# A hybrid encoder layer on one core: operands on 128-byte starts, meta rows in one operand, attention stage rearranged

## The reference

```python
h = concatenate([meta, x])                       # 16 + 512 rows
n = rmsnorm(h)
proj = n @ w_in                                  # 1024 x 3912: rq rk rv rg dq dk dv iq ik iw
ret = silu(rg) * groupnorm(retention(rope(rq), rope(rk), rv))     # 4 heads of 128, chunk-causal decay
isc = sum_h iw_h * relu(rope(iq_h) @ rope(ik))                    # indexer, 8 heads of 64
att = softmax over the 128 keys with the highest isc, 8 heads of 128; then @ w_uv
h  += concatenate([ret, att]) @ w_out            # 1024 x 1024
m = rmsnorm(h)
# PEER: product keys choose 16 of 128 x 128 experts for each of 8 heads and each row
h  += sum_e gelu(m . u_e) * gate_e * v_e
out = rmsnorm(h)[16:]
```

## Time and profile before

| | us |
|---|---|
| runs | 1708.06 (1706.65 to 1708.62) |
| profiled execution | 1707.09 |
| its span, first to last instruction | 1705.3 |
| mean granted TensorE clock | 0.997 |
| projection, to about | 235 |
| retention, attention, output, FFN norm, to about | 400 |
| routing with 24 up tiles, to about | 610 |
| up tiles, to | 1172 |
| down tiles, to | 1697 |

### The profile page before, as it was taken

The page is one execution under the profiler, slowest core; times in us unless marked ns, Lnnn a source line. Parts: engine busy times, 40 slices in busy tenths (PEclk is TensorE's granted clock), DMA queues, the critical chain, the costliest instruction groups (busy, mean ns, idle before and its releaser), DMA issues.

```text
span 1705.3 us, 23289 instructions
## 1 busy us (share of the span) xinstructions
PE 1681.4 (99%) x7773; PEld 1382.8 (81%) x7773; DVE 1102.3 (65%) x2966; ACT 576.7 (34%) x900; POOL 918.8 (54%) x855
## 2 busy tenths in 40 slices
PE   9999998999999999999999999999999999999998
PEld 8867876788888888888888888888888888888886
DVE  4269867456788854444444444434788888888887
ACT  5343235244323222222222222224333333333333
POOL 3654300005433037777777777763777777767710
PEclk9999999999999999999999999999999999999999
DMA  5322141044769444444456444455999999999991
GB/s 177 107 64 74 37 101 51 13 149 174 263 236 315 148 149 148 143 148 143 142 166 232 144 147 143 142 167 189 386 390 369 374 367 357 379 372 361 375 337 53
DMA packets 183250, 351.04 MB, mean 206 GB/s; under 512 B 35664, under 2 KB 118992, under 8 KB 183024
## 3 DMA queue, kind: packets, MB, share of 16 engines
q1 hardware_dynamic: 118400, 255.47, 44.5%
q0 software_dynamic: 34816, 67.41, 11.0%
q10 hardware_dynamic: 29952, 27.28, 4.9%
HBM read 289.04 MB, written 61.02 MB: 205 GB/s over the span
## 4 chain that ended last, share of the span: by engine, by line
PE 80%; DVE 2%; issue 2%; POOL 1%; ACT 1%; DMA 0%; DVEq 0%; POOLq 0%; ACTq 0%
PE psum L274 25%; PE psum L276 25%; PE psum L275 25%; PE psum L1078 1%; PE psum L1086 1%; PE psum L1100 1%; POOL ts_lo_wq L1623 1%; PE psum L1785 1%; PE psum L1129 1%; DVE att_masked L1341 0%; POOL cand L2034 0%; POOL ts_lo_u L1623 0%; DVE mixed L1325 0%; PE psum L1114 0%; PE psum L1142 0%
## 5 line engine op out<-in xcount | busy, mean ns | idle before, releaser
L2436 POOL DMA_INDIRECT gate_map<-gate_total,gate_at x384 | 403.6, 1051 | 200.7 <-DVE same_expert L2131 110.1
L274 PE MATMUL psum<-x_hi,ts_hi_u 128*128 128x512 f32 x1024 | 399.0, 390 | 1.8 <-POOL ts_lo_u L1623 1.1
L276 PE MATMUL psum<-x_hi,ts_lo_u 128*128 128x512 f32 x1024 | 398.4, 389 | 0.0
L275 PE MATMUL psum<-x_lo,ts_hi_u 128*128 128x512 f32 x1024 | 398.4, 389 | 0.0
L1623 DVE TENSOR_TENSOR ts_lo_u<-ts_raw_u,ts_hi_u 128x1024 fp32r<-128x1024 f32 x116 | 142.2, 1226 | 336.7 <-ACT ts_hi_u L1618 336.6
L274 PE MATMUL psum<-v_hi,c_hi 128*128 128x512 f32 x768 | 298.8, 389 | 0.0
L275 PE MATMUL psum<-v_lo,c_hi 128*128 128x512 f32 x768 | 298.8, 389 | 0.0
L276 PE MATMUL psum<-v_hi,c_lo 128*128 128x512 f32 x768 | 298.8, 389 | 0.0
L1618 ACT ACTIVATE ts_hi_u<-ts_raw_u 128x1024 fp32r<-128x1024 f32 x128 | 135.4, 1058 | 394.2 <-PE psum L276 394.2
L2331 ACT ACTIVATE v_hi<-v_raw 128x1024 fp32r<-128x1024 f32 x128 | 135.8, 1061 | 314.3 <-PE psum L276 314.3
L2424 POOL DMA_INDIRECT sparse_rows<-in_peer_v,v_row x128 | 159.4, 1245 | 126.1 <-DVE sparse_more L2166 36.4
(11 more groups left out here) (270 smaller groups left out, 2310.8 us busy)
## 6 DMA issues: line engine op xcount, KB each, us to landing
ts_raw_u<-in_peer_u SPq DMA_DIRECT2D x128, 512.0 KB, 3.6
v_raw<-in_peer_v SPq DMA_DIRECT2D x128, 512.0 KB, 6.0
gate_map<-zeros SPq DMA_DIRECT2D x32, 768.0 KB, 6.8
act_in<-up_acts SPq DMA_DIRECT2D x128, 192.0 KB, 5.7
gate_in<-gate_map SPq DMA_DIRECT2D x128, 192.0 KB, 6.6
up_acts<-ut_out_u ACTq DMA_DIRECT2D x104, 192.0 KB, 1.9
raw_in<-in_w_in SPq DMA_DIRECT2D x56, 256.0 KB, 2.7
ts_raw_wq<-in_peer_wq SPq DMA_DIRECT2D x16, 512.0 KB, 5.0
```

Source lines behind the costliest of these rows:

```text
L274: nc.tensor.matmul(out, l_hi, r_hi, start=first, stop=False)
L275: nc.tensor.matmul(out, l_hi, r_lo, start=False, stop=False)
L276: return nc.tensor.matmul(out, l_lo, r_hi, start=False, stop=last)
L2436: nc.gpsimd.indirect_dma_start(gate_cells, bass.IndirectOffsetOnAxis(places["gate_at"][:, b, j:j + 1], 0), dn.total[:, b, j:j + 1], None). ...
```

## The change

1. Starts: small filler tensors (`fill_line`) and other shapes make every fp32r operand begin at a multiple of 128 bytes: h_hi, h_lo and rk_t lose their meta columns ([.., 512] instead of 528), and the meta part of rk_t moves into an unused part of sel_bias (rk_m).
2. Meta rows: one operand meta_both holds the 16 high and the 16 low columns side by side. A meta output is two matmuls per k: both parts by w_hi (32 output rows), the high part by w_lo (16 rows). The two groups of rows are rotated alike (tables and scales have both) and are added by a matmul against `fold`, two stacked 16 x 16 unit matrices, where a transpose stood; in the retention of the meta keys both groups are kept (rows 0 to 31 of the decays), so the sum is made by the product.
3. Output projection: two tiles of k per step for blocks 0 and 1 (steps 12 to 19, 20 to 27), three for block 2 (28 to 33), by `out_step`. w_out units 7 to 15 are split one per step, in VectorE's list from step 3, in ScalarE's from step 2.
4. Retention roots: no Sqrt. VectorE makes a first guess from the bits (two operations), GpSimd three Newton steps of four operations, then -mean x root (two more); ScalarE normalises (Identity with scale and bias) in steps 3, 5, 7, 8, VectorE gates one step later. ScalarE loads the Sqrt table at step 32 for the FFN norm.

```diff
+        def fill_line(name, used, c=None, side=None):
+            sb(name, [P, -used % LINE // 4], c=c, side=side)
+        fill_line("edge", LINE - SB_TOP % LINE, side="right")
+        fold = sb("fold", [META_ROWS, META_ROWS])
...
+            fill_line("final_rest", 32 + 64, rows_ctx)
...
-                rk_t=sb_high("rk_t", [P, RET_HEADS, ROWS], c=high),
+                rk_t=sb_high("rk_t", [P, RET_HEADS, FRAMES], c=high),
...
+                rest=fill_line("dk_t_rest", 4 * ROWS, stream),
...
-                hi = sb("h_hi", [P, KT, ROWS], F32R, c=c2)
-                lo = sb("h_lo", [P, KT, ROWS], F32R, c=c2)
+                hi = sb("h_hi", [P, KT, FRAMES], F32R, c=c2)
+                lo = sb("h_lo", [P, KT, FRAMES], F32R, c=c2)
...
+            def meta_product(bank, k, s, w):
+                nc.tensor.matmul(psum[0:META_ROWS, bank, 0:w], meta_both[:, k], ws.hi[:, s, 0:w], start=(k == 0), stop=False)
+                return nc.tensor.matmul(psum[0:META, bank, 0:w], meta_both[:, k, 0:META], ws.lo[:, s, 0:w],
+                                        start=False, stop=(k == KT - 1))
...
+                    if b == NB:
+                        last = nc.tensor.matmul(out, rows_in, fold[:, 0:cols], start=True, stop=True)
...
+    def out_step(p, n):
+        return DSA_HEADS * (p + 1) + 4 + n // (2 if p < LAST - 1 else 3)
...
+        def refine_roots(g):                              
+            hs = HEAD_GROUPS[g]
+            y, v, t = rstd[:, hs], var[:, hs], ab["ret_step"][:, hs]
+            pool.wait_ge(guessed, 2 * g + 2)
+            at = ROOT_STEPS * g
+            for x in range(NEWTON):
+                nc.gpsimd.tensor_tensor(t, y, y, ALU.mult).then_inc(newton, 1)
+                pool.wait_ge(newton, at + 4 * x + 1)
...
         nc.gpsimd.memset(ret_scores[:, :, 0, :], 0.0).then_inc(padded, 1)
+        refine_roots(0)
         for i in range(UNITS):
+            if i == 3:
+                refine_roots(1)
...
+        def guess_roots(g):
+            hs = HEAD_GROUPS[g]
+            dve.wait_ge(var_done, g + 1)
+            nc.vector.tensor_scalar(halved[:, hs], var[:, hs].bitcast(U32), 1, None, ALU.logical_shift_right).then_inc(guessed, 1)
+            dve.wait_ge(guessed, 2 * g + 1)
+            nc.vector.tensor_scalar(rstd[:, hs].bitcast(U32), halved[:, hs], -1.0, ROOT_GUESS, ALU.mult, ALU.add).then_inc(guessed, 1)
...
-        def ret_sqrt(g):
-            hs = HEAD_GROUPS[g]
-            act.wait_ge(var_done, g + 1)
-            nc.scalar.activation(rstd[:, hs], var[:, hs], ACT.Sqrt).then_inc(root, 1)
+        def normalize(h):
+            act.wait_ge(newton, ROOT_STEPS * (2 if h == LAST_HEAD else 1))
+            for b in range(NB):
+                nc.scalar.activation(mixed[:, b, h * P:(h + 1) * P], sums[:, h, b * P:(b + 1) * P], ACT.Identity,
+                                     bias=ab["ret_step"][:, h, b:b + 1], scale=rstd[:, h, b:b + 1]).then_inc(normed, 1)
...
+            if i in NORMED_AT:
+                normalize(NORMED_AT.index(i))
+            if i == UNITS:
+                nc.scalar.activation(ab["unused"][:], ident[:, 0:1], ACT.Sqrt)
...
-            for u in range(2 * i - 11, 2 * i - 9):
-                if EARLY_W <= u < 2 * KT:
-                    split_hi(nc, act, ws, u, seen[u], 512)
+            if EARLY_W <= i + 5 < 2 * KT:
+                split_hi(nc, act, ws, i + 5, seen[i + 5], 512)
```

More of the change, by code:

```diff
@@ L90, in tables @@
             t[:, b] = full[b * P:(b + 1) * P]
-        t[:META, NB] = full[FRAMES:]
+        for g in range(META_PARTS):
+            t[g * META:(g + 1) * META, NB] = full[FRAMES:]
         out[name] = t
@@ L97, in tables @@
     decay = np.zeros((P, RET_HEADS, FRAMES), f)
-    decay_meta = np.zeros((META, RET_HEADS, FRAMES), f)
+    decay_meta = np.zeros((META_ROWS, RET_HEADS, FRAMES), f)
+    fold = np.tile(np.eye(META, dtype=f), (META_PARTS, META_PARTS))
     for h in range(RET_HEADS):
         decay[:, h] = np.where(seen, gamma[h] ** np.abs(n - m), 0.0) * RET_DIM ** -0.5
-        decay_meta[:, h] = gamma[h] ** (n + META - np.arange(META)[:, None]) * RET_DIM ** -0.5
+        for g in range(META_PARTS):
+            decay_meta[g * META:(g + 1) * META, h] = (
+                gamma[h] ** (n + META - np.arange(META)[:, None]) * RET_DIM ** -0.5)
     out["decay"] = decay
     out["decay_meta"] = decay_meta
+    out["fold"] = fold
     out["ident"] = np.eye(P, dtype=f)
@@ L505, in _ @@
                 load_unit(sp, ws, u, in_unit(io, u))
-            sp.dma_start(xm, io["meta_tokens"]).then_inc(meta_in, 16)
+            for g in range(META_PARTS):
+                sp.dma_start(xm[g * META:(g + 1) * META], io["meta_tokens"]).then_inc(meta_in, 16)
+            sp.dma_start(fold[:], io["fold"]).then_inc(fold_in, 16)
             sp.dma_start(rope128[:], io["rope128"]).then_inc(tables_in, 16)
@@ L529, in turn @@
                 tiles = 2 if name == "misc" else 4
+                if b == NB:
+                    pe.wait_ge(fold_in, 16)
                 for t in range(tiles):
-                    last = nc.tensor.transpose(psum[:, 4 + n % 2, t * P:t * P + r], rot[0:r, n % 2, t * P:(t + 1) * P],
-                                               ident[0:r, 0:r])
+                    cols = turned_columns(name, b)
+                    out, rows_in = psum[:, 4 + n % 2, t * P:t * P + cols], rot[0:r, n % 2, t * P:(t + 1) * P]
+                    if b == NB:
+                        last = nc.tensor.matmul(out, rows_in, fold[:, 0:cols], start=True, stop=True)
+                    else:
+                        last = nc.tensor.transpose(out, rows_in, ident[:])
                 last.then_inc(rot_turned, 1)
@@ L950, in mix_rows @@
     projected = sem("out_projected")
-    x_in = [sem(f"x_res_in{b}") for b in range(NB)]
+    x_in = sem("x_res_in")
     added = sem("out_added")
@@ L1002, in cols, with out_tiles_at, out_done_at @@
         return slice(ORDER[p] * P, (ORDER[p] + 1) * P)
-    def filler(i):
-        p, s = divmod(i - (DSA_HEADS + 3), DSA_HEADS)
-        return (p, s) if 0 <= p < LAST else (None, None)
+    def out_step(p, n):
+        return DSA_HEADS * (p + 1) + 4 + n // (2 if p < LAST - 1 else 3)
+    def out_tiles_at(i):
+        return [(p, n) for p in range(LAST) for n in range(2 * KT) if out_step(p, n) == i]
+    def out_done_at(i):
+        return [(p, half) for p in range(LAST) for half in range(2) if out_step(p, KT + half * HALF + HALF - 1) == i]
     def opens_block(i):
@@ L1145, in turn_dv_meta @@
         def turn_dv_meta():
-            nc.tensor.transpose(psum[:, META_T_BANK, 0:META], st["dv"][0:META, 0], ident[0:META, 0:META]).then_inc(dv_turned, 1)
+            nc.tensor.matmul(psum[:, META_T_BANK, 0:META], st["dv"][0:META_ROWS, 0], fold[:, 0:META], start=True, stop=True).then_inc(dv_turned, 1)
         def weigh_dv_meta():
@@ L1406, in refine @@
             dve.wait_ge(ffn_root, g + 1)
-            refine_rstd(nc, dve, refined, 2 + g, rstd_f[:, ps], mean[:, ps], ab["step"][:, ps])
+            refine_rstd(nc, dve, refined, g, rstd_f[:, ps], mean[:, ps], ab["step"][:, ps])
         def scale_rows(p):
@@ L1459, in vector @@
                 variance(1)
[L1460 to L1472 removed]
+                guess_roots(1)
+            if i - 1 in NORMED_AT:
+                gate_head(NORMED_AT.index(i - 1))
+            if EARLY_W <= i + 4 < 2 * KT:
+                split_lo(nc.vector, dve, ws, i + 4, 512)
+            for p, half in out_done_at(i - 1):
+                add_rows(p, half)
         reciprocal_roots(0)
```

168 lines of the change are left out of this document (83 added, 85 removed).

## The result

The kernel after takes **1695.07 us** (1694.0 to 1696.27), beside 1707.62 for the kernel before in runs between its own: a ratio of 0.9927, 95% interval 0.9909 to 0.9944, clear of 1 though small. The forecast was 1626.0, 1603 to 1649. It is faster, but of the 82 us forecast 12.5 came, and the time is that of the first rival (1696). The profiled execution took 1696.27 us, its span 1694.3.

What follows compares the result with a forecast made beforehand. It took TensorE as the bound, the up and down products limited by one matmul's cost. Savings of 57.3 + 3.6 + 0.5 + 2.5 + 10.5 + 4.9 + 6.7 - 3 - 1 = 82.0 us gave 1626 us, range 1603 to 1649.

Steps and rivals of the forecast that it cites:

- the first rival: All fp32r matmuls: alignment does nothing, the 13.3 ns belong to fp32r; 1696 us, chance 10%.
- Where the 32 columns go: fp32r matmuls: operands starting off 128 bytes touch 17 blocks instead of 16, which makes 226.7 ns instead of 213.3.
- The new pitch: Aligned fp32r matmuls of 512 columns: 216.0 ns each, between bounds of 213.3 and 226.7.
- The give-backs of 3 and 1 us: Savings returned: 3 us (0 to 10) in routing for VectorE, 1 us (0 to 23) in the down stage for DMA.
- rival 2: Down stage stays at its old pace, bound by DMA or VectorE; 23 us back, 1648 us, chance 9%.
- Meta rows: Input projection: three meta outputs of 24 matmuls become 16 each; -4.9 us.
- VectorE's list before the first output product: Attention, 255 to 290 us: VectorE's work sets when output products start; 5.8 us off, 3.4 ahead, taken as -2.2.
- The clock drop: After the wait before the first output product: half clock for 3.4 us goes with that gap; -1.7 us, other bound 0.
- Spreading the tiles: Attention steps 12 to 33: output tiles two or three per step cover the bare steps' waits; -1.8 of 2.7 us.
- The root table: FFN norm: ScalarE's root table loaded at step 32 instead of before ffn_sqrt, 1.28 us; taken as -1.0.
- Costed at nothing: Attention: ScalarE's 16 normalisations (nearest row 1.1 us) and GpSimd's two chains (up to 6.4 us each) covered, 0 us.
- Rival 3: Slower: TensorE's two operand streams get in each other's way, both starting at 0 costing 5.05 ns more; 1726 us, chance 5%.

Runs made afterwards that it cites:

- the small kernel: Separate kernel, TensorE alone: series of 72 fp32r matmuls of 512 columns at the layer's SBUF addresses; 226.7 ns at after's up-stage addresses, 231.7 at before's projection addresses.
- the third small kernel: Separate kernel, TensorE alone: matmul width varied at the up stage's operand addresses, plus plain float32 and bf16; fp32r 226.7 ns at 512 columns, bf16 215.8.
- the late splits: Kernel after with w_out units 7 to 15 split six steps later, from step 9 on VectorE and step 8 on ScalarE; 1692.07 us, ratio 0.9908.
- the bunched kernel: Kernel after with output tiles of blocks 0 to 2 back in four steps of each eight, w_out splits two per step; 1697.07 us, ratio 0.9933.

## Why the prediction was wrong, step by step

**The step that failed is "Where the 32 columns go".** It saw rightly that 13.3 ns, 32 columns' time, are in each matmul beyond its columns, and gave them to a 17th block of 128 bytes. They are a fixed cost of an fp32r matmul. The prediction had the row that says so: 328 columns at 150.0 ns and 512 at 226.65 differ by 76.7 ns, exactly 184 / 2.4, the fixed cost's number. It took the 512 columns from the projection instead, 231.7, since the 328 were there too, and found 81.7, nearer the blocks' 80.0. But the 231.7 held 5 ns that the 328-column row did not have, from the operands' distance. It wrote that both rows have "some 4 ns more than either count explains" and went on. That is a wrong reading for the 328 columns: the blocks leave 3.3 ns over there, while the fixed cost gives (328 + 32) / 2.4 = 150.0, the row itself. And a rest of 5 ns at 512 columns cannot choose between two counts 3.3 ns apart. The new pitch, 216.0, had no better ground: its 2.7 ns came from the earlier trace rows, where one plain float32 matmul was read as two.

With it fall the terms that rest on it. Up and down products: -57.3 forecast, 0 measured. Query products: -3.6 and -0.5, 0. Output projection: -2.5, none; its distance even went from 192 (229.0 in the small kernel, 228.8 in the earlier trace rows) to 384 (232.5 there; the medians of its three lines are 232 to 233). Input projection: -10.5 or -7.2, about -1.5 to -2.1 (the projection with the distance broken again, by the medians and by its own length), for another reason. The give-backs of 3 and 1 us had nothing to give back; DMA at 390 GB/s in the down stage is the old backlog, at the old pace, so rival 2 was not put to the test.

The Trainium skill, "TensorE: Matmul & The Clock Gate", section "Wait — 56ns, not 53.3ns?", gives 215.7 ns for 512 columns of bf16; the third small kernel has 215.8. The prediction had weighed it as the better bound for fp32r; fp32r has 226.7. "SBUF — State Buffer", section "Operand start alignment", asks for a multiple of the element size and says that this is about legality, not speed, so it leaves the time open. At the layer's row lengths the runs show 0.7 ns at most between starts at 0 and 96; with rows of 2176 and 640 bytes they show 8.2. On the distance between two operands the page says nothing.

**Meta rows**: -4.9 forecast; 3.2 by the ratios, 3.7 by the first retention score, 4.1 to 4.5 by the projection's own length. Right in its mechanism, and 0.4 to 1.7 us too large.

**VectorE's list before the first output product**: taking 5.8 us off and putting 3.4 ahead was the working, net -2.4, taken as -2.2. From the first retention score to the first output product the profiles take 62.5 us before and 60.3 after, -2.2. With the old roots put back it is 64.8, 4.5 more; with the late splits 58.0, 2.3 less. So the mechanism is shown in both halves, but each was sized 1.1 to 1.3 us too large, and the net came out right because the two misses cancel: luck.

**The clock drop** did not go as forecast, because a gap stays: TensorE waits 1.06 us for x_lo before the first output product (timeline, then stretches of the kernel after).

```profile
280.66 0.50 PE L1190 MATMUL psum<-ident,att_probs 128*128 128x128 f32 x3
282.22 0.55 PE L293 MATMUL psum<-whi_out,x_hi 128*128 128x512 f32 x1 [1.06 <-DVE x_lo L1459]
282.57 0.63 PE L294 MATMUL psum<-wlo_out,x_hi 128*128 128x512 f32 x1
```

```profile
282.00:284.00 2.00, 1.78 (x5) 1.44 (x6) 0.63 (x2) 0.32 (x2) 0.20 (x1) 0.63 0.00 0
284.00:286.00 2.00, 2.00 (x10) 1.70 (x9) 0.00 (x0) 0.20 (x1) 0.00 (x0) 0.52 0.00 0
286.00:290.00 4.00, 4.00 (x24) 3.21 (x24) 1.80 (x5) 1.11 (x3) 0.20 (x1) 1.00 0.36 131
```

For 3.4 us the granted clock is 0.5, 1.2 GHz, and the matmuls last 0.63 us in place of 0.39. It is there in two of the three profiles of the kernel after and absent in the third, whose marks behind it are 1.5 us earlier with the same 1.1 us wait; the two profiles with late splits have it neither. The mean granted clock of each run tells how often. Of the kernel after's 14 runs nine have 0.999 and took 1693.9 to 1695.1 us, the profile without the drop among them; five have 0.996 to 0.998 and took 1695.8 to 1698.0, both profiles with it among them. No run of the kernel before that has a clock on record is above 0.998 (39 beside the experiments). So the 1.7 us came in about two runs of three, although the gap stayed; what decides it from run to run is open. The profile laid beside the old one above is one of the five.

**Spreading the tiles**: -1.8 forecast, 1 to 2.6 measured (the bunched kernel alone, and beside the old roots; 2.3 in the profiles). Right, and the waits that came back are those named.

**The root table**: -1.0 forecast, 0. The load had cover: ScalarE was ahead of VectorE there.

**Costed at nothing**, and rightly: ScalarE's normalisation takes 1.64 us per head, not 1.1, and GpSimd's second chain 4.7 us of the 6.4 allowed, most operations of 0.2 (the first 5.0); ScalarE never waits for it (timeline):

```profile
259.48 0.20 POOL L1122 TENSOR_TENSOR ret_step<-ret_rstd 128x4 f32<-128x4 f32 x1 [1.24 <-DVE ret_rstd L1400]
...
263.55 0.60 POOL L1132 TENSOR_SCALAR ret_step<-ret_step 128x4 f32<-128x4 f32 x1
```

```profile
266.26 1.64 ACT L1589 ACTIVATE mixed<-ret_sums,ret_step,ret_rstd 128x128 f32<-128x128 f32 x4
```

The sum of what was measured, by medians: attention and output 7.9 (the clock's share in it), meta rows 3.2 to 3.7, projection's distance 1.5, together 12.6 to 13.1, beside 12.5 to 13.3 for the whole. Rival 1 said 1696 with 10%. Its mechanism was right: the 13.3 ns belong to fp32r. That its number was within 1 us is part luck: attention and output gave 1.2 more than its 6.7, the meta rows about 1 less than its 4.9, and the projection's distance was not in it. Rival 3's observation, that 512 columns cost 5 ns more in the projection stage for the way its two streams stand, was right too, but it is the operands' distance and not their starts, and this change left it good where it mattered: the up stage at a bad one takes 1712.

## What to carry to other kernels

A number that fits a mechanism (544 columns = 17 blocks) is one equation; find a row in which the rivals differ by more than the row's own unexplained rest, and take both widths from the stage where each is cleanest. A term that is 70% of a forecast and has no row that shows its end state deserves a chance near even, not 76%. For fp32r products of 512 columns, lay out the operands so that each stationary start less its moving start is a multiple of 256 bytes, with moving rows of 2048 bytes, and check it for every k. With other row lengths measure first: at 2176 and 640 bytes a distance of 0 gave 228.4 ns once and 236.6 once.

## What the hardware did that was not expected

An fp32r matmul costs 32 columns' time more than its own from 328 to 512 columns (226.7 ns at 512, against 215.8 for bf16), and about 111 ns at 224 columns or fewer. Two fp32r operands of 512-column matmuls at a bad distance cost 2 to 8 ns more per matmul (229.0 to 234.2 against 226.7), at 256 columns nothing, plain float32 and bf16 none; with rows of 2176 and 640 bytes it was 236.6 at a distance that elsewhere is good, so there is more to it than the distance. A new row of 512-column matmuls often ran at 223 to 237 ns for some ten of them before its 226.7 set in. The same kernel with the same wait of 1.06 us got full clock behind it or half clock for 3.4 us. And a filler of 128 bytes between two tensors made a tuned kernel 17 us slower.
